# First modulation columns: which row groups TensorE takes and which VectorE takes, and in what order

## The reference, cut to what matters

```python
cond = jax.nn.silu(c)                                   # (1, 1024)
mod = (cond @ ada_w[l] + ada_b[l]).reshape(B, 6, D_MODEL)[:, :, None, :]
shift1, scale1, gate1 = mod[:, 0], mod[:, 1], mod[:, 2]
...
u = rmsnorm(x, norm_mix[l]) * (1.0 + scale1) + shift1
aq, ak, av, bq, bkv, biq, bik, biw, cq, ck, cv, g = split_cols(u @ w_in[l])
```

## Time and profile before

| | us |
|---|---|
| median of 3 runs | 2781.55 |
| lowest and highest | 2779.86, 2782.89 |
| the profiled execution | 2778.82 |
| its span | 2777.0 |
| TensorE matmul busy | 2642.5 (95%) |
| VectorE busy | 1476.4 (53%) |
| ScalarE busy | 1123.9 (40%) |
| mean granted TensorE clock | 0.974 |

### The profile page before, as it was taken

The page is one execution under the profiler, slowest core; times in us unless marked ns, Lnnn a source line. Parts: engine busy times, 40 slices in busy tenths (PEclk is TensorE's granted clock), DMA queues, the critical chain, the costliest instruction groups (busy, mean ns, idle before and its releaser), DMA issues.

```text
span 2777.0 us, 33464 instructions
## 1 busy us (share of the span) xinstructions
PE 2642.5 (95%) x13597; PEld 2177.3 (78%) x13597; DVE 1476.4 (53%) x2501; ACT 1123.9 (40%) x1845; POOL 408.7 (15%) x295
## 2 busy tenths in 40 slices
PE   7998899999999999998898999999999999999997
PEld 5775576888888987786886878889788886888887
DVE  5286867255332289798863643333734744642334
ACT  4355344244332234545653443323543543532223
POOL 0122223101000035443010110000000100200000
PEclk7999899899999999999999999999999999999999
DMA  7333223432333333212421233333231341233331
GB/s 245 109 97 94 61 77 106 112 108 84 93 97 92 98 84 84 69 39 84 129 84 38 74 95 97 92 98 93 70 84 31 115 120 46 80 96 93 97 92 61
DMA packets 468970, 251.31 MB, mean 90 GB/s; under 512 B 15582, under 2 KB 463666, under 8 KB 468815
## 3 DMA queue, kind: packets, MB, share of 16 engines
q1 hardware_dynamic: 466260, 242.56, 30.5%
q0 software_dynamic: 1840, 5.59, 0.7%
q10 hardware_dynamic: 715, 1.01, 0.1%
HBM read 247.00 MB, written 2.13 MB: 90 GB/s over the span
## 4 chain that ended last, share of the span: by engine, by line
PE 78%; DVE 14%; ACT 6%; issue 1%; POOL 0%; DMA 0%; SPq 0%; POOLq 0%; DVEq 0%; ACTq 0%
PE ps L935 19%; PE ps L931 19%; PE ps L933 19%; PE ps L867 2%; PE ps L863 2%; PE ps L865 2%; DVE ps L2464 2%; PE ps L891 1%; DVE w_r L2337 1%; PE ps L1412 1%; PE ps L881 1%; PE ps L883 1%; PE ps L1095 1%; ACT wh L1556 1%; DVE arena_f L2552 1%
## 5 line engine op out<-in xcount | busy, mean ns | idle before, releaser
L931 PE MATMUL ps<-XH,wh 128*128 128x512 f32 (+2 forms) x1896 | 770.8, 407 | 11.8 <-ACT arena_f L1746 3.7
L935 PE MATMUL ps<-XH,w_r 128*128 128x512 f32 (+2 forms) x1896 | 754.4, 398 | 5.8 <-DVE w_r L2337 4.0
L933 PE MATMUL ps<-XL,wh 128*128 128x512 f32 x1776 | 709.6, 400 | 2.8 <-DVE XL L2870 2.8
L2337 DVE TENSOR_TENSOR w_r<-w_f,wh 128x1024 fp32r<-128x1024 f32 (+1 forms) x316 | 378.7, 1201 | 565.5 <-ACT wh L1556 565.2
L1556 ACT ACTIVATE wh<-w_f 128x1024 fp32r<-128x1024 f32 (+2 forms) x407 | 411.1, 1012 | 374.8 <-PE ps L935 209.9
L931 PEld LDWEIGHTS ps<-XH,wh 128*128 128x128 f32 (+2 forms) x1896 | 359.8, 190 | 120.9 <-issue 19.8
L935 PEld LDWEIGHTS ps<-XH,w_r 128*128 128x128 f32 (+2 forms) x1896 | 358.1, 189 | 94.9 <-DVE w_r L2337 6.6
L933 PEld LDWEIGHTS ps<-XL,wh 128*128 128x128 f32 x1776 | 336.0, 189 | 85.7 <-issue 4.6
L933 PE MATMUL ps<-arena_r,wh 128*128 128x512 f32 (+1 forms) x936 | 342.9, 366 | 0.0
L931 PE MATMUL ps<-arena_r,wh 128*128 128x512 f32 (+1 forms) x726 | 264.9, 365 | 1.4 <-ACT wh L1556 1.4
L935 PE MATMUL ps<-arena_r,w_r 128*128 128x512 f32 (+1 forms) x726 | 259.8, 358 | 6.2 <-DVE w_r L2337 6.2
(11 more groups left out here) (388 smaller groups left out, 3774.7 us busy)
## 6 DMA issues: line engine op xcount, KB each, us to landing
w_f<-in_mlp_w SPq DMA_DIRECT2D x126, 512.0 KB, 4.1
w_f<-in_w_ff SPq DMA_DIRECT2D x63, 512.0 KB, 4.0
w_f<-in_w_in SPq DMA_DIRECT2D x49, 512.0 KB, 3.8
w_f<-in_ada_w SPq DMA_DIRECT2D x35, 512.0 KB, 3.9
w_f<-in_even_w_in SPq DMA_DIRECT2D x35, 512.0 KB, 3.8
w_f<-in_odd_w_in SPq DMA_DIRECT2D x23, 512.0 KB, 3.8
w_f<-in_even_w_out SPq DMA_DIRECT2D x16, 512.0 KB, 4.1
w_f<-in_xa_w_v SPq DMA_DIRECT2D x16, 512.0 KB, 4.1
```

Source lines behind the costliest of these rows:

```text
L931: e.matmul(b, hi[:, k, :], xh, start=u.first and k == 0, stop=False)
L933: e.matmul(b, hi[:, k, :], xl, start=False, stop=False)
L935: last = e.matmul(b, lo[:, k, :], xh, start=False, stop=u.final and k == u.kc - 1)
L2337: e.tensor_tensor(flat(u, 1), flat(u, 0), high_flat(u).bitcast(F32), ALU.subtract).then_inc(dve.sem, dve.up("low", u.n))
```

## The change

MOD_ROWS becomes (3, 5, 7): TensorE takes three of the eight k, VectorE five (0, 1, 2, 4, 6). On TensorE, the groups of k=3 and k=5 stand behind each other ahead of the norm's sum, the sums group follows the strips and waits for k=6, and the group of k=7, whose blocks arrive last, comes behind the sums group and writes into the same bank, columns 32 to 47. On VectorE, k=0, 1, 2 come ahead of the packs' copies, k=4 ahead of the squares and k=6 behind them; at the end there are two additions in place of one, both behind TensorE's third group. SyncE's wait for the slots of k=7 is now for that third group; the wait for the slot of k=6 is still for VectorE.

```diff
-MOD_ROWS = (2, 3)
+MOD_ROWS = (3, 5, 7)
@@ SyncE
                     if old.name == "mod":
-                        w.wait_ge(dve, "mod sum", old.m)
+                        if old.m // 2 in MOD_ROWS:
+                            w.wait_ge(pe, "mod rows", MOD_ROWS.index(old.m // 2))
+                        else:
+                            w.wait_ge(dve, "mod sum", old.m)
@@ TensorE
             mod_rows(rows_bank, 0)
+            mod_rows(rows_bank, 1)
             rms_sums("mix", KC)
...
-            mod_rows(rows_bank, 1)
             b, freed = lin.take("mod")
             w.wait_ge(*freed)
             for h in range(2):
-                w.wait_ge(dve, "mod sum", 2 * (KC - 1) + h)
+                w.wait_ge(dve, "mod sum", 2 * (KC - 2) + h)
...
             last.then_inc(pe.sem, pe.up("mod"))
+            mod_rows(b, 2)
@@ VectorE
-            mod_sum(0)
+            for k in range(3):
+                mod_sum(k)
             for n in range(1, 5):
                 turn_pack(n)
-            mod_sum(1)
+            mod_sum(4)
             for k in range(KC):
                 add_square("mix", k)
-            for k in range(2, KC):
-                if k not in MOD_ROWS:
-                    mod_sum(k)
+            mod_sum(6)
...
+            b = lin.of("mod")
             w.wait_ge(dve, "mod part")
-            w.wait_ge(pe, "mod")
-            e.tensor_tensor(mod, lin.of("mod")[:, 0:16], mod, ALU.add).then_inc(dve.sem, dve.up("mod", 15))
+            w.wait_ge(pe, "mod rows", 2)
+            e.tensor_tensor(mod, b[:, 0:16], mod, ALU.add).then_inc(dve.sem, dve.up("mod parts"))
+            w.wait_ge(dve, "mod parts")
+            e.tensor_tensor(mod, b[:, 32:48], mod, ALU.add).then_inc(dve.sem, dve.up("mod", 15))
             lin.free(dve, "mod")
```

## The result

The changed kernel takes 2784.26 us (median of 20 runs, 2781.52 to 2790.18); the kernel before, over 20 runs, takes 2779.72 us. The ratio is 1.0019 with a 95% interval of 1.0012 to 1.0025, which is +5.3 us (3.3 to 6.9); the plain difference of the two medians is 4.5 us. The interval lies wholly above 1, so the change is slower, by a little less than the 5.6 us that the prediction took as the least that can be told from no change. The profiled execution has a span of 2783.1 us where the kernel before had 2777.0, so 6.1 us more.

A forecast was written before the change was run, and what follows sets the result against it. TensorE's groups at 1.2 GHz were taken to end the stage: 1.33 later start + 1.35 lower clock - 3.24 filled idle + 6.84 fourth group + 0.21 addition = 6.49, so +6.5 on 2781.55 gives 2788.1 us; range 2783.5 to 2791.2.

The forecast's parts named there:

- Late start of the first group: TensorE's first group, now k=3, waits for its first block to land: start at 23.40 instead of 22.07, +1.33 us.
- First two groups: TensorE's k=3 and k=5 take 6.52 and 6.84 us, the clock falling at 23.72, and end at 36.76.
- rival (1): Part of TensorE's new groups runs at 2.4 GHz, saving 1.4 or 1.65 us: +5.0, 2786.5 us; chance 0.22.
- Norm and strips, sums, third group: On TensorE these take 4.21, 6.84 and 6.84 us behind 36.76, ending at 54.65.
- VectorE's cover: VectorE ends the squares near 34.0 and k=6 at 36.4, before TensorE needs them, 2.8 and 4.6 us to spare.
- The second addition: At VectorE's end, two additions in place of one, both behind TensorE's third group: +0.21 us.
- SyncE's queue: Loads behind k=7's slots wait until 54.65; worst landing 71.5 against use at 73.4, hidden by 1.9 us, nothing added.
- Rival (2): Project products start cold for longer, their clock rising later: 1.9 us more, 2790.0 us; chance 0.15.
- Rival (4): Delay swallowed because something behind the first products already waited for another engine or a load: 2781.6 us; chance 0.04.
- rival (5): VectorE was the bound after all, so its two blocks fewer gain 2.4 us: 2779.1 us; chance 0.01.
- Rival (3): Unbroken TensorE work keeps the whole stretch at 2.4 GHz, groups 3.42 us: -5 to -7 us, 2775.6; chance 0.03.
- the rule: Skill page: a busy TensorE goes to 2.4 GHz; the prediction rejected it for these one-column groups, keeping 1.2 GHz.

The follow-up runs named there:

- e1: Changed kernel with only k=3 and k=5 on TensorE and k=7 given to VectorE behind k=6; 2777.65 us, ratio 0.9993 to the kernel before.
- e7: Kernel before with the sums group issued a second time into unread columns, VectorE waiting for the second; 2788.62 us, ratio 1.0027.
- e2: Kernel before with both TensorE groups of rows (k=2, k=3) ahead of the norm's sum; 2775.13 us, ratio 0.9978.
- e6: Changed kernel with k=2, 5, 7 on TensorE in place of 3, 5, 7; 2784.23 us, ratio 1.0016 to the kernel before.
- e10: Kernel before, unchanged, profiled a second time; one run, 2777.89 us.
- e3: Kernel before with 64 moving columns in place of one in the groups of rows and sums; 2783.34 us, ratio 1.0004.
- e12: Changed kernel with 128 moving columns, k=2, 4, 7 on TensorE and k=7 between strips and sums; 2774.16 us, ratio 0.9984 to the kernel before.
- e8: Kernel before with both groups of rows ahead of the norm and 128 moving columns in rows and sums; 2773.74 us, ratio 0.9972.
- e9: Changed kernel with 128 moving columns in place of one; 2774.84 us, ratio 0.9978 to the kernel before.
- e5: Kernel before with both groups of rows ahead of the norm and 64 moving columns; 2775.67 us, ratio 0.9981.
- e11: e5 word for word, profiled a second time; one run, 2774.66 us.
- e4: Changed kernel with 64 moving columns in place of one; 2784.99 us, ratio 1.0014 to the kernel before.

## Why the prediction was right, and where it was off

The forecast was +6.5 us, the measurement +5.3 (3.3 to 6.9), and the sign was right, by the mechanism that was forecast: e1 takes the third group of rows away and e7 adds a fourth group alone, and both move the first product by what one group takes at 1.2 GHz. As a time, 2788.1 stood 3.8 us above the 2784.26 measured; 1.8 us of that is the kernel before itself, whose median was 2781.55 over 3 runs and 2779.72 over 20. By its steps:

- **Late start of the first group.** Predicted +1.33, measured 23.59-22.07 = +1.52. The first block of k=3 landed at 23.54, 0.14 us later than in the kernel before, though this execution's transposes stood 0.4 to 0.6 us later.
- **First two groups.** Predicted 6.52+6.84 = 13.36 us, measured 36.55-23.59 = 12.96. The clock fell at 24.4, not at 23.72. This is the term whose size was off: I read a moment that scatters over 3.4 us from one execution as if the kernel set it. With a fall at 26 to 27, as in e1, e2, e6, e7 and e10, the first group would end near 27 to 28 and k=5 would wait for its landing. e1, with the same order up to the sums and the fall at 25.9, shows what that takes off: 11.97 us for the two groups, another 1.0 less, where rival (1) had priced it with 1.4. Whether it happened in many of the changed kernel's 20 runs is not shown, and nothing asks for it: the profile's 6.1 us and my 6.5 both lie within the runs' interval.
- **Norm and strips, sums, third group.** Predicted 4.21, 6.84, 6.84; measured 4.22 (36.55 to 40.77), 6.85 (to 47.62) and, by the same length, an end at 54.47 against the 54.65 of the sum. e7 measures the fourth group by itself: +6.80 at the first product.
- **VectorE's cover.** Squares ended at about 34.0, k=6 at 36.4, both as worked out, and TensorE waited for neither. The copies of the packs ended near 24.4.
- **The second addition.** 54.69 to 54.90, the predicted 0.21; the idle time ahead of the first product grows from 2.17 to 2.38.
- **SyncE's queue.** It waited 17.7 us on TensorE's third group, and the next loads were issued at 54.62. ScalarE rounded these two weights at 73.68, with no wait for a load. The changed kernel's waits of SyncE's queue:

```profile
SPq L805 <- PE ps L972: 17.7, 1, 17.7
```

The landings of that line's loads from 50 to 80:

```profile
DMA to landing us min/median/max: 3.7/3.9/5.8
```

And ScalarE's timeline:

```profile
73.68 2.00 ACT L1560 ACTIVATE wh<-w_f 128x1024 fp32r<-128x1024 f32 x2
```

The margin was larger than I had it, about 60.4 to 73.7: the longest landing was 5.8 us and not 16.8, with nothing moved by DMA from 51.0 to 54.6.

Rival (2), a longer cold start, seems to come true by a third: the clock rose at 61.95, 5.0 us after the first product where it was 3.8, and the first bias tiles stood at 71.27 against 64.47, 6.8 us later. But this distance scatters too: it is 3.5 us in e10, the same kernel as before, 3.3 in e7, where the product comes later still, and 5.3 in e3. So it is not shown to be the change's doing. The span is 6.1 us longer, so 0.7 us of the 6.8 came back behind the bias tiles, within what the executions differ by: from the first product to the end of the span, twelve of the fourteen profiles lie between 2725.2 and 2727.5 us, e12 at 2726.7 among them, e8 at 2728.3 and e3 at 2731.6. e3's clock was low at places where the others' was not: from 206.3 to 214.3 the mean was 0.79, and in the kernel before, e7 and e8 it was 1.00 in the same stretch behind the first product. Why is open. Rival (4) is ruled out by these distances and by e7, rival (5) by e1, where VectorE has two blocks more and the first product is earlier, and by VectorE's 9.37 us of waiting. (Its chance of 0.01, a gain, was counted among the 0.64 for slower.)

Rival (3), 3 in 100, did not occur: the changed kernel's clock stood at 1.2 GHz from 24.4 to 61.9 while TensorE had no idle time up to 54.5. Two windows of the changed kernel, with the columns of the earlier trace rows:

```profile
24.50:61.50 37.00, 34.62 (x138) 30.04 (x138) 18.89 (x27) 12.56 (x18) 2.69 (x5) 0.50 0.61 200
61.50:62.00 0.50, 0.50 (x2) 0.41 (x2) 0.47 (x2) 0.50 (x1) 0.00 (x0) 0.55 0.00 0
```

The Trainium skill, page "TensorE: Matmul & The Clock Gate", Part 1, says that activity releases the throttle. The changed kernel's trace does not agree: 30.1 us of unbroken work, groups of one column with the norm and the strips among them, stayed at 1.2 GHz from 24.4 to 54.5. The traces of e8 and e12 agree, where the clock rose at 41.0 and 37.8 inside a group of 128 columns. My rejection of the rule rested on the right rows; what I had missed is that the kernel can be edited so that its groups run at 2.4 GHz, as in e9.

## What to carry to other kernels

Before work is moved to the engine with idle time, look at which of the two ends the stage and at what one unit costs on each: a k of two blocks is 2.4 us on VectorE and 6.84 us on TensorE at 1.2 GHz, and 3.2 us of idle time on the path do not pay for a fourth group. Filling that idle time with what was there already (e2) made the kernel 6.1 us faster, part of it because a later fall of the clock, worth nothing ahead of a wait, counts once the groups stand on the path. Where matmuls of one column run at the low clock, a wider moving operand is worth a run: it costs no instructions, and with 128 columns each group of e9 took about 3 us less than at 1.2 GHz. In e8 and e12 a wait had let the clock fall, and the group behind it took 5.4 to 5.6 us.

## What the runs showed of the hardware that I had not expected

- With one column, TensorE's clock fell from 2.4 to 1.2 GHz at a moment that the kernel's order does not fix: 23.7 to 27.1 us over seven executions, two of them of the same kernel (23.7 and 26.7). In four it fell inside a group, in three in the idle time behind one.
- At 128 moving columns a group of 32 instructions takes 3.67 us from start to start of the next (e9, 36.46 to 40.13), against 6.84 us with one column at 1.2 GHz and 3.64 us with its tail at 2.4 GHz (e6). Less a tail of 0.15, the estimate for the latter is 3.49 us, so the wide product adds about 0.2 us to a group.
- With 64 columns TensorE stayed at 2.4 GHz through two groups, norm and strips in two executions (e5, e11), and in a third (e4) the clock fell inside a group. What tells these apart stays open; the third came behind 1.77 us of idle time.
- The scatter of one kernel's time goes with its granted clock. Of the 89 executions of the kernel before beside the experiments, the 11 with a mean clock of 0.975 took 2774.7 to 2778.7 us, and the 25 with 0.972 took 2781.3 to 2784.0. So a median of 3 runs can be off by some microseconds, as the first one here was.
